# Layer two's four memory blocks moved from the program's start to the seam between the layers

## What is computed

```python
for l in range(DEPTH):                       # DEPTH = 2
    h, s = hgrn2_mixer(...) if l % 2 == 0 else gla_mixer(...)   # in-projection, recurrence, out-projection
    x = post_norm(x, h, ln_g[l, 0], ln_b[l, 0])
    c = memory_cross_attention(x, mem_ks[l], mem_vs[l], xattn_w_q[l], xattn_w_o[l])
    x = post_norm(x, c, ln_g[l, 1], ln_b[l, 1])
    m = grouped_moe(x, router_w, router_bias, moe_w_gate[l], moe_w_up[l], moe_w_down[l])
    x = post_norm(x, m, ln_g[l, 2], ln_b[l, 2])
```

```python
def memory_kv(mem, w_kv):                    # mem (1, 256, 1024), w_kv (1024, 2048), once per layer
    kv = (mem @ w_kv).reshape(B, M, 2, X_HEADS, X_HEAD_DIM)
    return kv[:, :, 0], kv[:, :, 1]
```

## Time and profile before

| | before |
|---|---|
| median of three runs | 1402.84 us |
| the profiled execution's span | 1402.6 us |
| TensorE busy | 97% |
| VectorE busy | 73% |
| ScalarE busy | 54% |
| mean DMA rate over the span | 249 GB/s |

### The profile page before, as it was taken

One profiled execution on the slowest core, in us unless ns is written; L12 is line 12 of the kernel. 1 busy time (PEld: TensorE's weight loads), 2 busy tenths in 40 slices (PEclk: granted clock), 3 DMA queues, 4 the chain that ended last, 5 costly groups with the idle time before them and its releaser, 6 DMA issues.

```text
span 1402.6 us, 19786 instructions
## 1 busy us (share of the span) xinstructions
PE 1354.3 (97%) x7719; PEld 1125.0 (80%) x7719; DVE 1024.1 (73%) x1102; ACT 756.8 (54%) x775; POOL 139.6 (10%) x209
## 2 busy tenths in 40 slices
PE   8999999999899999999999999999899999999996
PEld 6789898779777788888887798779777788888884
DVE  4545776683558889898988356783658889898986
ACT  4444743333444677676777353332434777676765
POOL 5200035400000000000000014200000000000000
PEclk9999999999999999999999999999999999999998
DMA  9766454524975699999993355434984699999981
GB/s 283 239 225 196 150 180 125 147 88 173 373 315 187 236 363 345 345 357 329 362 342 121 120 180 185 132 122 170 373 321 163 256 369 340 351 341 342 359 324 38
DMA packets 101427, 349.49 MB, mean 249 GB/s; under 512 B 6304, under 2 KB 32432, under 8 KB 72160
## 3 DMA queue, kind: packets, MB, share of 16 engines
q1 hardware_dynamic: 96480, 331.90, 65.5%
q0 software_dynamic: 4864, 16.45, 3.4%
HBM read 330.75 MB, written 17.57 MB: 248 GB/s over the span
## 4 chain that ended last, share of the span: by engine, by line
PE 79%; DVE 10%; ACT 4%; DMA 3%; issue 2%; POOL 2%; SPq 0%; DVEq 0%; ACTq 0%; POOLq 0%
PE ps L1824 64%; DMA att_kt<-in_cache_mem_v 2%; PE ps L2179 1%; PE ps L2389 1%; PE ps L2202 1%; DVE mix_s L1548 1%; PE ps L1833 1%; PE ps L2190 1%; DVE x L1269 1%; PE ps L1832 1%; DVE x L1266 1%; PE ps L1919 1%; PE ps L2332 1%; DVE x L1232 1%; PE ps L2333 1%
## 5 line engine op out<-in xcount | busy, mean ns | idle before, releaser
L1202 DVE TENSOR_TENSOR w_lo<-raw,w_hi 128x2048 fp32r<-128x2048 f32 x64 | 146.1, 2294 | 133.5 <-ACT w_hi L793 133.5
L1824 PE MATMUL ps<-w_hi,xt_hi 128*128 128x512 f32 x576 | 230.1, 400 | 6.1 <-DVE w_lo L1206 2.3
L1824 PE MATMUL ps<-w_hi,xt_lo 128*128 128x512 f32 x576 | 226.0, 392 | 0.0
L793 ACT ACTIVATE w_hi<-raw 128x2048 fp32r<-128x2048 f32 x64 | 121.8, 1913 | 148.2 <-PE ps L1824 77.6
L1824 PE MATMUL ps<-w_lo,xt_hi 128*128 128x512 f32 x512 | 200.9, 392 | 0.0
L1206 DVE TENSOR_TENSOR moe_lo<-moe_in_raw,w_hi 128x2048 fp32r<-128x2048 f32 x72 | 164.2, 2290 | 22.6 <-ACT w_hi L800 22.6
L1206 DVE TENSOR_TENSOR w_lo<-raw,w_hi 128x2048 fp32r<-128x2048 f32 x72 | 164.8, 2291 | 16.6 <-ACT w_hi L800 16.1
L800 ACT ACTIVATE w_hi<-moe_in_raw 128x2048 fp32r<-128x2048 f32 x72 | 138.1, 1918 | 56.4 <-PE ps L1824 56.4
L800 ACT ACTIVATE w_hi<-raw 128x2048 fp32r<-128x2048 f32 x72 | 137.5, 1912 | 14.8 <-PE ps L1824 14.8
L1824 PE MATMUL ps<-xt_hi,w_hi 128*128 128x320 f32 x448 | 138.6, 309 | 0.2
L1824 PE MATMUL ps<-xt_hi,w_lo 128*128 128x320 f32 x448 | 138.4, 309 | 0.0
(11 more groups left out here) (399 smaller groups left out, 2585.9 us busy)
## 6 DMA issues: line engine op xcount, KB each, us to landing
raw<-in_moe_w_gate SPq DMA_DIRECT2D x48, 1024.0 KB, 4.9
moe_in_raw<-in_moe_w_down SPq DMA_DIRECT2D x48, 1024.0 KB, 4.8
moe_in_raw<-in_moe_w_up SPq DMA_DIRECT2D x32, 1024.0 KB, 5.0
raw<-in_moe_w_up SPq DMA_DIRECT2D x32, 1024.0 KB, 5.5
raw<-in_hgrn_w_in SPq DMA_DIRECT2D x16, 1024.0 KB, 5.7
raw<-in_cache_mem_k SPq DMA_DIRECT2D x16, 1024.0 KB, 6.4
moe_in_raw<-in_moe_w_gate SPq DMA_DIRECT2D x16, 1024.0 KB, 5.4
raw<-in_moe_w_down SPq DMA_DIRECT2D x16, 1024.0 KB, 4.9
```

The source lines that it names most:

```text
L793: nc.scalar.activation(hi_at(hi_slot(k)), raw_at(r), ACT.Copy).then_inc(w_high, 1)
L1202: nc.vector.tensor_tensor(lo_at(slot_of(k)), raw_at(slot_of(k)), hi_at(hi_slot(k)).bitcast(F32), ALU.subtract).then_inc(w_low, 1)
L1824: ins = mm(out, lhs, rhs, start=start and n == 0, stop=stop and n == 2, skip_group_check=shared)
```

## The change

- Layer one's four memory blocks stay at the start; layer two's four (blocks 18 to 21 in the new count) stand between layer one's last experts and layer two's first in-projection. The weights' chunks follow in the same order.
- The split memory rows (`mem_hi`, `mem_lo`, 1 MB each) are overwritten by the mixer meanwhile. SyncE stores them to two internal DRAM tensors `mem_rows_kept_hi` and `_lo` at the start, behind the tokens' loads and ahead of the fourth chunk, and loads them back into the experts' `xn_hi` and `xn_lo` behind the last experts' loads, ahead of layer two's first chunk.
- The token transposes stand one memory block sooner: `X_AFTER = (0, 1, 2, 3)`.
- At the seam the two first memory blocks are cut in pieces between the sums and the tiles' transposes, the 30 `keep_busy` matmuls are gone (layer two's own end keeps its nine), and the first in-projection block runs as a whole behind the fourth memory block instead of tile by tile.
- ScalarE and VectorE split one chunk before the tiles' sums and one between the tiles, and ScalarE copies the four blocks out to a staging area in the experts' `raw`; GpSimd stores them.

```diff
-KV_BLOCKS = 2 * 4
+KV_BLOCKS = (4, 4)
-X_AFTER = (1, 2, 3, 4)
+X_AFTER = (0, 1, 2, 3)
...
             sp.dma_start(x[:, 0:2, :], a["x_prompt"][0].rearrange("(t p) c -> p t c", p=P)).then_inc(x_in, 16)
             sp.dma_start(x[0:64, 2, :], a["x_sample"].rearrange("b t c -> (b t) c")).then_inc(x_in, 16)
+            sp.wait_ge(xt_l, 8)
+            for part in range(2):
+                sp.dma_start(mem_rows_kept[part], st_kv[("mem_hi", "mem_lo")[part]][:].bitcast(F32)).then_inc(mem_in[part], 16)
...
+                if l == 1:
+                    for part in range(2):
+                        sp.wait_ge(mem_in[part], 32)
+                        sp.dma_start(late_mem[part].bitcast(F32), mem_rows_kept[part]).then_inc(mem_in[part], 16)
                 dense(done, in_end(l), groups)
...
@@ ScalarE, the end of layer one's experts @@
+                nc.scalar.preload_act_table_set("natural_log_exp_and_others")
                 if l == 0:
                     splits[0] += NH
-                nc.scalar.preload_act_table_set("natural_log_exp_and_others")
+                    split(splits[0], groups)
+                    splits[0] += 1
                 tile_sums(l, 0, nl * SIDES + 14)
                 tile_sums(l, 1, nl * SIDES + 16)
                 if l == 0:
+                    kv_block_out(BLOCKS0)
                     turned(4, 0)
                 tile_sums(l, 2, nl * SIDES + 18)
                 if l == 0:
                     turned(4, 1)
+                    split(splits[0], groups)
+                    splits[0] += 1
                     turned(4, 2)
+                    for db in range(BLOCKS0 + 1, first_block(1)):
+                        kv_block_out(db)
...
@@ TensorE, the seam @@
-                    keep_busy(14, 4)
+                    for part in range(2):
+                        pe.wait_ge(mem_in[part], 48)
+                    pe.wait_ge(evac[0], db // 2)
+                    memory_chunk(db, groups, 0, 0, 4)
+                    for n in range(4):
+                        side(last + 1, "s", n, last * SIDES + 13 + n, (7, 6, 2, 3)[n])
+                    memory_chunk(db, groups, 1, 0, 4)
+                    for n in range(4, 6):
+                        side(last + 1, "s", n, last * SIDES + 13 + n, (7, 6)[n - 4])
                     turn_next(0)
...
-                    keep_busy(7, 2)
-                    first_values(0, 0)
+                    pe.wait_ge(evac[1], (db + 1) // 2)
+                    memory_chunk(db + 1, groups, 0, 0, 4)
+                    pe.wait_ge(s["read"], last * SIDES + 18)
                     turn_next(1)
...
+                    for late in range(db + 2, first_block(1)):
+                        dense(late, groups, "N", 2)
```

More of the change, by code:

```diff
@@ L406, in hi_at, with mem_parts, kv_staged @@
             return w_hi[:, r] if r < NH else st_moe["hi"][:, r - NH]
+        late_mem = [st_moe[part][:, 0:2, :].rearrange("p t (k m) -> p (t k) m", m=MEM) for part in ("xn_hi", "xn_lo")]
+        def mem_parts(db):
+            return (st_kv["mem_hi"], st_kv["mem_lo"]) if db < KV_BLOCKS[0] else late_mem
+        def kv_staged(db):
+            if db < KV_BLOCKS[0]:
+                return st_kv["out"][:, db % 2]
+            return st_raw["raw"][:, 0, 2 * (db % 2):2 * (db % 2) + 2, :]
         def high_low_values(l):
@@ L731, in _ @@
                 load_ln(3 * l)
+                for db in range(BLOCKS0, first_block(l)):
+                    kv_store(db)
                 tables(l)
@@ L946, in _ @@
             split_ahead(-1, None)
-            for db in range(KV_BLOCKS):
+            for db in range(KV_BLOCKS[0]):
                 par = db % 2
@@ L1367, in _ @@
                 m = st_mix[l]
-                if l == 0:
-                    for par in range(2):
-                        dve.wait_ge(kv_out[par], 16 * KV_BLOCKS // 2)
+                for par in range(2):
+                    dve.wait_ge(kv_out[par], kv_outs(l))
+                for part in range(2):
+                    dve.wait_ge(mem_in[part], 32)
                 def scan(hh):
@@ L1812, in _ @@
                     samples_pad(xt_lo[:, :, PROMPT:NT].bitcast(F32))
-                    splits[0] += NH
+                    for db in range(BLOCKS0 + 1, first_block(1)):
+                        split_ahead(db, groups)
+                else:
+                    for n in range(6):
+                        side(0, "s", n, nl * SIDES + 13 + n, (7, 6, 0, 1, 2, 3)[n])
+                    for t in range(TILES):
+                        tile_scale(l, t)
         @block.tensor
@@ L1838, in tile_products, with memory_products, memory_chunk @@
                 return three(ps[:, 4 * par + t, :], w_hi[:, rh, kc, :], w_lo[:, r, kc, :], xt_hi[:, kt, toks], xt_lo[:, kt, toks], start, stop, False)
+            def memory_products(db, r, rh, kc, kt):
+                hi, lo = mem_parts(db)
+                for t in range(2):
+                    toks = slice(t * P, (t + 1) * P)
+                    ins = three(ps[:, 4 * (db % 2) + t, :], w_hi[:, rh, kc, :], w_lo[:, r, kc, :], hi[:, kt, toks], lo[:, kt, toks], kt == 0, kt == KT - 1, False)
+                return ins
+            def memory_chunk(db, groups, half, first, last):
+                k = chunk_no(db) + half
+                if first == 0:
+                    pe.wait_ge(w_low, at(k + 1, groups, GCH))
+                for kc in range(first, last):
+                    ins = memory_products(db, slot_of(k), hi_slot(k), kc, 4 * half + kc)
+                if last == 4:
+                    ins.then_inc(w_used, 1)
             def dense(db, groups, mode, tiles=TILES):
@@ L2403, in _ @@
                 visit(nl, False, True)
-                keep_busy(9, 0)
-                for n in range(6):
-                    side(nl + 1, "s", n, nl * SIDES + 13 + n, (7, 6, 0, 1, 2, 3)[n])
+                if l == 1:
+                    keep_busy(9, 0)
+                    for n in range(6):
+                        side(nl + 1, "s", n, nl * SIDES + 13 + n, (7, 6, 0, 1, 2, 3)[n])
+                else:
+                    last = nl
                 groups = nl + 1 if groups is None else groups + nl + 1
                 if l == 0:
-                    db = first_block(1)
+                    db = BLOCKS0
                     def turn_next(t):
```

86 lines of the change are left out of this document (48 added, 38 removed).

## The result

The changed kernel takes 1410.27 us, the median of 4 runs (1408.1 to 1410.43), beside 1403.22 us for the kernel before in 4 runs on the same chip (1402.1 to 1403.86). The ratio is 1.0041, with a 95% interval of 1.0029 to 1.0053: 4.1 to 7.4 us slower. (It isn't the quotient of the two medians, which is 1.0050, or 7.05 us; that lies inside the interval.) The forecast was 1410.4.

The account below looks back on a forecast made before the run. TensorE, busy 97% of the span, was taken as the bound. Seam -8.1, fourth chunk +8.1, eighth chunk -0.7, last transposes +4.9 and clock +3.4 gave +7.6 us, 1410.4 us; range 1402.5 to 1414.5.

Parts of the forecast that it names:

- The seam: Between the layers: 9.57 us of TensorE waste replaced by moved work, less 1.5 us of new waits; 8.1 us won.
- The load back: At the seam: the 2 MB loaded ahead of layer two's first chunk cost nothing, with slack of 1 us or so.
- The fourth chunk: At the start: behind 2 MB of stores it lands at 32.5, so TensorE starts at 36.8, not 28.7; 8.1 us lost.
- The eighth chunk: At the start: the wait TensorE has for this chunk before 52.66 goes; 0.7 us won.
- The last transposes: Ahead of the in-projection: no memory block covers ScalarE's and VectorE's work on the last two groups; 4.9 us lost.
- The clock: Behind both new gaps at the start: the granted clock falls, 1.7 us each; 3.4 us lost.
- a smaller store: Rival at the start: stores move at 400 GB/s or so and clock falls once, or gap half as long; 1405.7–1407.5; chance 0.15.
- even: Rival at the start: stores take 5.1 us, fourth chunk costs 3.9, clock falls in neither gap; 1402.8 us; chance 0.13.
- the stores ride beside the loads: Rival at the start: stores and loads share no limit, fourth chunk lands by 24.4; 1399.0 to 1400.7 us; chance 0.07.
- the load back is late: Rival at the seam: layer two's first chunk lands after 747.3, adding 2 to 5 us; 1412 to 1415; chance 0.10.
- The sum: Whole kernel: -8.1 + 8.1 - 0.7 + 4.9 + 3.4 = +7.6 us, 1410.4 on the median of the runs.
- signs named for being wrong: Fourth chunk landing before 28, the clock staying at 1.00, or the seam winning less than 6.5 us.

Follow-up runs that it names:

- experiment 7: Changed kernel with transposes behind memory blocks 0 and 2 only and the stores behind the eighth chunk's load: 1395.68 us, ratio 0.9937; run again 1396.12 us, 0.9944.
- experiment 9: On experiment 7, ScalarE and VectorE split layer two's fourth chunk behind the first tile's norm instead of ahead of it: 1392.58 us, ratio 0.9919.
- experiment 8: On experiment 7, the memory's 2 MB loaded back twice, the second time behind the first's landing, ahead of layer two's first chunk: 1395.79 us, ratio 0.9944.
- experiment 1: Changed kernel with the fourth weight chunk issued ahead of the two stores instead of behind them: 1405.07 us, ratio 1.0005.
- experiment 5: Kernel before with the 2 MB of stores added ahead of the fourth chunk, read by nobody: 1412.09 us, ratio 1.0059.
- experiment 11: Changed kernel's start with 2 MB of unused loads ahead of the fourth chunk, the stores behind the eighth chunk's load: 1411.68 us, ratio 1.0055.
- experiment 2: Changed kernel with the token transposes behind memory blocks 0 and 2, none behind the last block: 1402.73 us, ratio 0.9990.
- experiment 6: Kernel before with the last two column groups' token transposes moved behind the last memory block: 1411.05 us, ratio 1.0047.
- Experiment 4: Changed kernel with unread float32 matmuls filling both waits at the start, six ahead of the fourth chunk, five ahead of the in-projection: 1408.23 us, ratio 1.0028.
- experiment 3: Changed kernel with the fourth chunk ahead of the stores and transposes behind memory blocks 0 and 2 only: 1396.3 us, ratio 0.9949.

## Why the prediction was right, step by step

The sign, the time and the mechanism held; some terms were off and cancelled.

- **The seam, -8.1**: 7.9 by the trace, 8 to 9 by the medians of experiment 7. The wait for the first tile was put at 1.3 and is 1.58, with the cause that was named (experiment 9); of 0.2 us for the third tile the changed kernel shows nothing.
- **The load back, 0**: right by the trace (ScalarE's splits stand where they stood relative to the end of the experts). The slack was put at 1 us or so for ScalarE. Experiment 8 bears that out or less (the chunk came 5.0 us later and ScalarE stood 4.84 us for it), but ahead of TensorE there are some 3.6 us, and a delay of 5 us cost 1.1 to 1.6. So the rival's price of 2 to 5 us was set too high.
- **The fourth chunk, +8.1**: the mechanism is shown by experiments 1, 5 and 7, the size was off: 5.8. The step that failed is the landing, set at 32.5 by the fifth and sixth chunks that follow it in the kernel before. That is the price of two loads (experiment 11: 33.1), and stores were assumed to cost the same; they landed it at 31.1, 1.4 us sooner. The other 0.9 us are the later start: TensorE wanted the chunk at 29.6 and not at 28.7, mostly since the second chunk came 0.7 us later in this execution.
- **The eighth chunk, -0.7**: the wait is gone.
- **The last transposes, +4.9**: 4.82, shown by experiments 2 and 6. It was the term read from the closest row: the same sequence of instructions, in the trace of the kernel before, with nobody waiting.
- **The clock, +3.4**: 4.9 in the profiled execution, 2.4 and 2.5 behind the two waits. Experiment 4 ties it to the idle time. The 1.7 us came from the one place in the kernel before where it could be seen, and by the matmuls' starts that place lost 1.6; two places were taken to lose as much, and lost more. Elsewhere the same waits lost 1.3 to 1.6 (experiments 1, 2, 5 and 6). The Trainium skill, "TensorE: Matmul & The Clock Gate", "What's actually happening", says that an idle array's clock is halved; the trace agrees for all eight waits of 3.49 us or more, and not for all shorter ones (below).
- **The rivals**: "a smaller store" had a part of the truth, as the landing came sooner than forecast, but at 31.1 it is nearer to the forecast's 32.5 than to the 28.4 of stores at 400 GB/s, and the clock fell twice; "even" and "the stores ride beside the loads" fall with experiment 5, "the load back is late" with experiment 8. None of the signs named for being wrong came.
- **The sum**: +6.95 in the terms as measured (-7.9 + 5.8 - 0.65 + 4.8 + 4.9) beside the +7.6 forecast. What the forecast had no term for took 1.1 off: +0.7 for the second chunk, -1.6 of clock that the profiled execution did not lose behind 922, and -0.2 at the waits for cached values. That gives +5.85 of the span's +6.1. That the sum came out so close is luck in part: the store was set 2.3 too high and the clock 1.5 too low, and the second chunk's landing (0.7 us) and the clock behind 922 (1.6 us) change from trace to trace.
- One reading was loose. A run's time is 1.7 to 1.8 us above its profiled span in nearly all runs (1410.43 and 1408.7 here), so the execution of span 1402.6 was above the median of the kernel before, not at it.

What the study adds: the losses aren't the price of moving the blocks. They come from two choices at the start, and without them the move is worth 0.6%, with one more change of order at the seam 0.8%.

## What to carry to other kernels

When a buffer has to be saved so that work can move, the place of the save in the queue decides: ahead of a load that the next product needs it cost its whole transfer less the slack of that load (8.0 us of delay, 5.8 of stall), and behind the last load that a free slot allows it cost nothing. When work is taken away from between a producer and its consumer, look in the old trace for the same chain of instructions without a waiter: its length was the new stall here (4.9 us read ahead, 4.82 in each of four traces). And add the clock behind each new wait of this size, 1.3 to 2.5 us here.

## What the runs showed of the hardware that was not expected

- **Stores cheaper than loads in a full queue**: the fourth chunk lands at 30.8 to 31.1 behind 2 MB stored (four traces), at 33.1 behind 2 MB loaded (one trace), and at 22.4 to 25.2 with neither (nine traces). Both are slower than 2 MB at the best window's 410 GB/s (5.1 us), if one goes by the kernel before (23.14): between 24 and 30 us the DMA engines are busy the whole time in the changed kernel's windows and move 212 to 287 GB/s. The stores aren't the cause of that: the kernel before, without them, moves 206 and 181 GB/s from 24 to 28 us at a busy share of 1.15. GpSimd has issued small constants until 24; that these are the cause was not tested.
- **The clock behind a wait is partly a matter of the execution.** The 2.09 us wait of the earlier trace rows stands in 13 traces unfilled. Behind it the clock fell in six (1.6 us each) and held in seven. At the second chunk it fell after 1.79, 2.07 and 2.14 us (experiments 5, 2 and 1) and held after 1.46 or less, in ten traces. It held once after 3.05 us (experiment 3) and fell after all eight waits of 3.49 to 8.12 us. By the matmuls' starts the loss was 1.3 to 1.6 us in fourteen cases and 2.0 to 2.5 in three. In experiment 11 it was 1.5 behind a wait of 8.12 us, since much of the low stretch lay inside the wait.
- **Half the clock is not half the speed here.** A 128x512 matmul starts every 0.43 us at the low level and every 0.23 us at the high one, 1.8 times and not twice, so the missing clock of the windows overstates the loss by a tenth (2.7 and 2.4 us).
- **The spread of this kernel's times is of that size.** The executions of one kernel lie some 4 us apart, with mean clocks that differ by 0.002 to 0.003, and 0.001 of 1400 us is 1.4 us.
